# The last item's expert output spread to its tokens on chip, the other items' rows added beside it

## What is computed

```python
logits = (xf @ w_router + b_router).astype(jnp.float32)
top_val, top_idx = lax.top_k(logits, TOP_K)
top_w = jax.nn.softmax(top_val, axis=-1)
comb = jnp.sum(jax.nn.one_hot(top_idx, N_EXPERTS) * top_w[..., None], axis=1)
for e in range(N_EXPERTS):
    hh = xf @ w_expert_in[e] + b_expert_in[e]
    gate = jnp.minimum(hh[:, :D_EXPERT], SWIGLU_LIMIT)
    lin = jnp.clip(hh[:, D_EXPERT:], -SWIGLU_LIMIT, SWIGLU_LIMIT)
    act = (lin + 1.0) * gate * jax.nn.sigmoid(SWIGLU_ALPHA * gate)
    y = y + comb[:, e:e + 1] * (act @ w_expert_out[e] + b_expert_out[e])
...
x = x + gate2(c) * y        # c: one row for the prompt, one for each sample
y_out = rmsnorm(x, final_norm_g)
```

## Time and profile before

| | |
|---|---|
| median of 3 runs | 1531.92 us (1530.77 to 1532.19) |
| the profiled execution, its own time | 1529.73 us |
| its span, first to last instruction | 1528.0 us |
| granted TensorE clock over the span, mean | 0.915 |
| TensorE busy | 1259.7 us, 82% |
| VectorE, ScalarE, POOL busy | 356.3, 307.9, 183.5 us |
| moved by DMA | 534.38 MB, 350 GB/s over the span |
| expert phase, slices of 38.2 us | DMA busy 9 tenths or more in each, 411 to 429 GB/s |

### The profile page before, as it was taken

How to read it: one execution, slowest core, us unless ns; L and a number is a source line. 1 busy time by engine, 2 the same in 40 slices (tenths; PEclk the granted TensorE clock), 3 DMA queues, 4 the chain that set the end, 5 groups by cost and what they waited for, 6 DMA issues and landing times.

```text
span 1528.0 us, 27699 instructions
## 1 busy us (share of the span) xinstructions
PE 1259.7 (82%) x10935; PEld 692.7 (45%) x10936; DVE 356.3 (23%) x756; ACT 307.9 (20%) x638; POOL 183.5 (12%) x300
## 2 busy tenths in 40 slices
PE   6999999999999789999954698496969666954694
PEld 3777887767887434444421243132423222421241
DVE  1023113333631322222211122121222112211123
ACT  3100122442100222222211122121212111211123
POOL 0240100100180001111000011000100000100010
PEclk9999999999999899999987699797989888987697
DMA  9876734999555388799999999999999999999994
GB/s 367 303 286 227 267 111 149 386 371 402 184 179 226 139 342 338 285 419 421 415 427 427 425 412 423 425 419 426 415 418 411 429 423 416 417 429 426 422 411 170
DMA packets 76681, 534.38 MB, mean 350 GB/s; under 512 B 6428, under 2 KB 7540, under 8 KB 49793
## 3 DMA queue, kind: packets, MB, share of 16 engines
q1 hardware_dynamic: 67330, 503.47, 80.5%
q0 software_dynamic: 8928, 29.54, 6.0%
q10 hardware_dynamic: 391, 0.93, 0.2%
HBM read 508.38 MB, written 28.09 MB: 351 GB/s over the span
## 4 chain that ended last, share of the span: by engine, by line
PE 56%; DMA 40%; DVE 2%; SPq 1%; issue 1%; ACT 0%; DVEq 0%; ACTq 0%; POOL 0%; POOLq 0%
DMA ring<-in_w_expert_in_dram 21%; PE ps L754 16%; PE ps L922 12%; DMA moe_ring<-in_w_expert_out_dram 11%; PE ps L946 9%; DMA moe_ring<-in_w_expert_in_dram 5%; PE ps L511 2%; PE ps L891 2%; PE ps L796 2%; PE ps L837 2%; PE ps L803 2%; PE ps L783 2%; DMA ring<-in_w_in_dram 1%; DMA ring<-in_w_ada_dram 1%; PE ps L558 1%; PE ps L637 1%
## 5 line engine op out<-in xcount | busy, mean ns | idle before, releaser
L922 PE MATMUL ps<-ring,xgT 128*32 128x512 f32 x2352 | 318.7, 664 | 179.0 <-DMA ring<-in_w_expert_in_dram 178.5
L754 PE MATMUL ps<-hT,ring 128*128 128x264 f32 x1152 | 268.8, 391 | 6.1 <-DMA ring<-in_w_in_dram 4.7
L754 PEld LDWEIGHTS ps<-hT,ring 128*128 128x128 f32 x1152 | 218.5, 192 | 59.4 <-issue 14.6
L922 PEld LDWEIGHTS ps<-ring,xgT 128*32 128x32 f32 x2352 | 66.2, 116 | 318.3 <-DMA ring<-in_w_expert_in_dram 185.5
L946 PE MATMUL ps<-moe_ring,actT 128*32 128x256 f32 x3136 | 181.7, 380 | 4.7 <-DMA moe_ring<-in_w_expert_out_dram 4.2
L1526 DVE TENSOR_TENSOR xg<-ps,sh_q 128x256 f32<-128x256 f32 x49 | 20.8, 425 | 554.9 <-PE ps L891 554.9
L1164 ACT ACTIVATE ostage<-ps,slots_w 32x256 f32<-32x256 f32 x196 | 91.6, 467 | 285.9 <-PE ps L946 284.1
L946 PEld LDWEIGHTS ps<-moe_ring,actT 128*32 128x32 f32 x3136 | 99.3, 110 | 86.1 <-issue 18.0
L922 PE MATMUL ps<-moe_ring,xgT 128*32 128x512 f32 x784 | 93.7, 595 | 21.3 <-DMA moe_ring<-in_w_expert_in_dram 21.3
L891 PE MATMUL ps<-rows,picked 128*32 128x256 f32 (+1 forms) x1200 | 81.8, 386 | 1.3 <-DVE picked L1481 1.3
L1156 ACT COPY actT<-ps 128x256 f32<-128x256 f32 x49 | 18.3, 373 | 306.7 <-PE ps L511 306.7
(11 more groups left out here) (285 smaller groups left out, 1135.3 us busy)
## 6 DMA issues: line engine op xcount, KB each, us to landing
ring<-in_w_expert_in_dram SPq DMA_DIRECT2D x96, 2048.0 KB, 12.3
moe_ring<-in_w_expert_out_dram SPq DMA_DIRECT2D x64, 2048.0 KB, 12.0
moe_ring<-in_w_expert_in_dram SPq DMA_DIRECT2D x32, 2048.0 KB
ring<-in_w_in_dram SPq DMA_DIRECT2D x18, 2048.0 KB, 12.1
ring<-in_w_ada_dram SPq DMA_DIRECT2D x12, 2048.0 KB, 8.7
ring<-in_state_ret_dram SPq DMA_DIRECT2D x8, 1024.0 KB, 10.8
vslot<-in_state_ret_dram SPq DMA_DIRECT2D x8, 1024.0 KB, 10.8
out_dram<-ring POOLq DMA_DIRECT2D x8, 1024.0 KB, 9.1
```

The costliest lines, as they stand in the source:

```text
L754: mm = nc.tensor.matmul(ps[:, j, 0:T], ring[s][:, k, j * P:(j + 1) * P], hT[:, k, :], start=(k == 0), stop=(k == KC - 1))
L922: mm = nc.tensor.matmul(side(0, g), xgT[:, a, j * SLOTS:(j + 1) * SLOTS], w[:, a, g * COL:(g + 1) * COL], start=False, stop=(j == 3 and a ...
```

## The change

The last item's output is no longer scattered to DRAM and read back. VectorE multiplies its four quarters in PSUM by the slots' weights and by the prompt's gates at once, into `gated` (32 slots by 1024), and TensorE spreads it to the tokens with one-hot matrices `slot_rows` (32 slots by token), which VectorE makes from the item's slot numbers. The sum of the 48 items before is loaded by POOL, not by SP, once their last scatter is in; VectorE multiplies it by the gates and adds it to x1 (`earlier_items`). For the sample tokens, whose gates differ from token to token, ScalarE's `ostage` of the last item is spread ungated, and VectorE multiplies the spread rows by `gate_sample`, which POOL loads early.

The gate matmul for the prompt moves ahead of `outward`, the one for the samples goes. The turned rows of x1 use PSUM bank 5 in place of 1; bank 5 holds the slot numbers of `pick`, so TensorE first waits for `slots_taken`. VectorE's order of the tail becomes add 0, add 1, variance 0, finish 0, variance 1, add 2, finish 1, variance 2, finish 2; ScalarE's stays, with a wait for `out_gated` ahead of `take_outward`.

```diff
@@ SP
-            items = sp.value_load(cum_i[0:1, E - 1:E], min_val=E, max_val=ITEMS)
-            for j in range(2):
-                sp.wait_ge(chunk_used[j], items)
-                sp.sem_inc(paced, 1)
-            sp.wait_ge(rows_free, items + 1)
-            sp.sem_inc(paced, 1)
-            for t, (t0, n) in enumerate(TILES):
-                sp.dma_start(y_in[t][0:n], moe_rows[t0:t0 + n]).then_inc(rows_in[t], 16)
@@ TensorE
-                        mm = turn(ps[0:n, (1, 6, 7)[g % 3], k * P:(k + 1) * P], xT[:, 4 * half + k, t0:t0 + n])
+                        mm = turn(ps[0:n, (5, 6, 7)[g % 3], k * P:(k + 1) * P], xT[:, 4 * half + k, t0:t0 + n])
...
+            pe.wait_ge(slots_taken, SLOT_STEPS * items + SLOT_STEPS)
             rows_turned_back(0, 3)
             turn_hidden(items - 1)
+            pe.wait_ge(hidden_taken, 2 * items + 2)
+            for h in range(2):
+                mm = nc.tensor.matmul(ps[:, h, :], const("selc", NB)[:, 0:P], gate_rows[:, h * COL:(h + 1) * COL], start=True, stop=True)
+            mm.then_inc(rows_spread, 1)
             outward(items - 1, last, True)
 
             pe.wait_ge(x1_copied, 6)
+            pe.wait_ge(out_gated, SIDES)
+            for t in range(2):
+                for h in range(2):
+                    mm = nc.tensor.matmul(ps[:, 3 + 2 * t + h, :], slot_rows[:, t * P:(t + 1) * P], gated[:, h * COL:(h + 1) * COL], start=True, stop=True)
+                mm.then_inc(rows_spread, 1)
+            pe.wait_ge(eo_taken, items + 1)
+            pe.sem_inc(paced, 1)
             for h in range(2):
-                nc.tensor.matmul(ps[:, h, :], const("selc", NB)[:, 0:P], gate_rows[:, h * COL:(h + 1) * COL], start=True, stop=True)
-            for h in range(2):
-                mm = nc.tensor.matmul(ps[0:TS, 6 + h, :], const("selc", NB)[:, TP:T], gate_rows[:, h * COL:(h + 1) * COL], start=True, stop=True)
-            mm.then_inc(gates_spread, 1)
+                mm = nc.tensor.matmul(ps[0:TS, (7, 2)[h], :], slot_rows[:, TP:T], ostage[:, h * COL:(h + 1) * COL], start=True, stop=True)
+            mm.then_inc(rows_spread, 1)
@@ ScalarE
             take_rows(3, 6)
+            act_e.wait_ge(out_gated, SIDES)
             take_outward(items - 1)
@@ VectorE
-            for j in range(2, CHUNKS):
+            for j in range(2):
                 dve.wait_ge(chunk_used[j], items)
             step(nc.vector.memset(small[:, 2:5], 0.0))
-            dve.wait_ge(gates_spread, 1)
+            step(cp(slot_f[:], slots_u[:, bass.ds(items - 1, 1)]))
+            for t, (t0, n) in enumerate(TILES):
+                step(ts(slot_rows[:, t0:t0 + n], const("iota", SLOTS)[:, 0:n], float(t0), slot_f[0:SLOTS, 0:1], ALU.add, ALU.is_equal))
+            gates = ps[:, 0:2, :].rearrange("p b n -> p (b n)")
+
+            def earlier_items(t):
+                n = TILES[t][1]
+                dve.wait_ge(rows_in, 48)
+                step(tt(y_in[t][0:n], y_in[t][0:n], gates if t < 2 else gate_sample[:], ALU.mult))
+                dve.wait_ge(x1_copied, 2 * t + 2)
+                step(tt(x1_rows[0:n, t, :], x1_rows[0:n, t, :], y_in[t][0:n], ALU.add))
+
+            dve.wait_ge(late_in, 32)
+            dve.wait_ge(rows_spread, 1)
+            for g in range(SIDES):
+                side = slice(SLOTS * g, SLOTS * (g + 1))
+                step(cp(gate_side[side], gates[side, g * QUARTER:(g + 1) * QUARTER]))
+            for t in range(3):
+                earlier_items(t)
+            dve.wait_ge(chunk_used[5], items)
+            for g in range(SIDES):
+                side = slice(SLOTS * g, SLOTS * (g + 1))
+                stt(gated[:, g * QUARTER:(g + 1) * QUARTER], ps[side, 2, 0:QUARTER], slots_w[side, bass.ds(items - 1, 1)],
+                    gate_side[side], ALU.mult, ALU.mult).then_inc(out_gated, 1)
+
             def add_rows(t):
-                n = TILES[t][1]
-                bank = 0 if t < 2 else 6
-                gates = ps[0:n, bank:bank + 2, :].rearrange("p b n -> p (b n)")
-                dve.wait_ge(rows_in[t], 16)
-                step(tt(y_out[t][0:n], y_in[t][0:n], gates, ALU.mult))
-                tt(y_out[t][0:n], y_out[t][0:n], x1_rows[0:n, t, :], ALU.add).then_inc(y_added, 1)
+                dve.wait_ge(rows_spread, t + 2)
+                if t < 2:
+                    tt(y_out[t][:], ps[:, 3 + 2 * t:5 + 2 * t, :].rearrange("p b n -> p (b n)"), x1_rows[:, t, :], ALU.add).then_inc(y_added, 1)
+                else:
+                    for h in range(2):
+                        cols = slice(h * COL, (h + 1) * COL)
+                        step(tt(y_out[2][0:TS, cols], ps[0:TS, (7, 2)[h], :], gate_sample[:, cols], ALU.mult))
+                    tt(y_out[2][0:TS], y_out[2][0:TS], x1_rows[0:TS, 2, :], ALU.add).then_inc(y_added, 1)
@@ POOL
             pool.dma_start(g_final[:], final_norm_g.unsqueeze(0).broadcast_to([P, D])).then_inc(late_in, 16)
+            pool.wait_ge(last_rows_ready, 2)
+            pool.dma_start(gate_sample[:], kept_rows[1, 1:NB]).then_inc(late_in, 16)
...
-            scatter(items - 1, None)
+            for j in range(2):
+                pool.wait_ge(chunk_used[j], items)
+                pool.sem_inc(paced, 1)
+            for t, (t0, n) in enumerate(TILES):
+                pool.dma_start(y_in[t][0:n], moe_rows[t0:t0 + n]).then_inc(rows_in, 16)
```

More of the change, by code:

```diff
@@ L277, in trunk_kernel @@
         y_in = [at(f"y_in{t}", [P, D], ring_at + 4096 * t) for t in range(3)]
+        gated = at("gated", [SLOTS, D], ring_at + 28672)
+        slot_rows = at("slot_rows", [SLOTS, T], ring_at + 24576)
+        slot_f = at("slot_f", [P, 1], ring_at + 24576 + size([SLOTS, T]))
+        gate_side = at("gate_side", [P, QUARTER], ring_at + 24576 + size([SLOTS, T]) + size([P, 1]))
+        gate_sample = at("gate_sample", [TS, D], h_at + size([P, D]))
         y_sq = [at(f"y_sq{t}", [P, D], ring_at + 12288 + 4096 * t) for t in range(3)]
@@ L356, in trunk_kernel @@
         last_rows_ready = sem("last_rows_ready")
-        rows_in, gates_spread = [sem(f"rows_in{t}") for t in range(3)], sem("gates_spread")
+        rows_in, rows_spread = sem("rows_in"), sem("rows_spread")
+        out_gated = sem("out_gated")
         y_added, y_squared, y_ready, y_stored = sem("y_added"), sem("y_squared"), sem("y_ready"), sem("y_stored")
@@ L1173, in take_rows @@
                     act_e.wait_ge(x1_turned, g + 1)
-                    nc.scalar.copy(x1_rows[0:n, t, half * COL:(half + 1) * COL], ps[0:n, (1, 6, 7)[g % 3], :]).then_inc(x1_copied, 1)
+                    nc.scalar.copy(x1_rows[0:n, t, half * COL:(half + 1) * COL], ps[0:n, (5, 6, 7)[g % 3], :]).then_inc(x1_copied, 1)
             act_e.wait_ge(moe_cleared, 32)
@@ L1568, in finish_rows @@
                 stt(y_out[t][0:n], y_out[t][0:n], small[0:n, 5 + t:6 + t], g_final[0:n], ALU.mult, ALU.mult).then_inc(y_ready, 1)
-            dve.wait_ge(late_in, 16)
             add_rows(0)
@@ L1573, in _ @@
             variance(0)
+            finish_rows(0)
+            variance(1)
             add_rows(2)
-            variance(1)
-            finish_rows(0)
+            finish_rows(1)
             variance(2)
-            finish_rows(1)
             finish_rows(2)
```

## The result

The changed kernel took 1540.92 us (median of 6, 1536.87 to 1543.34) against 1532.05 for the kernel before (6 runs, 1530.65 to 1533.03): ratio 1.0058, 95% interval 1.0044 to 1.0072. It is slower, as forecast, but by 8.9 us where 5.8 were forecast, and 0.3 us over the upper end of the range. The profiled execution took 1541.72, with a span of 1539.8 (before 1528.0).

The account below looks back on a forecast made before the run. The weight stream was taken to bound the kernel until 1501.4; behind it, loads, VectorE's order and half-clock one-hot pairs, then sums, roots and store, ended at 1533.8 against 1528.0: 5.8 us more, so 1537.7, range 1533.5 to 1540.6.

Parts of the forecast that it names:

- tail: Stretch from VectorE's copy of the last slot weights to the span's end; forecast at 38.1 us.
- first operation on the loaded rows: VectorE's start on the earlier items' rows, once all POOL loads land, at 1503.9.
- gated rows: VectorE's products of the last item, behind all operations on earlier rows; ready at 1513.0.
- The four products: VectorE's gated products of the last item's four quarters, 4 x 0.4 = 1.6 us.
- The pair with its hand-over: TensorE's first pair of one-hot matmuls at half clock, 3.4 us, with 0.1 for handing over.
- The six operations with their hand-over: VectorE's work on three tiles of earlier rows ahead of the gated products, 7.5 us.
- what shifts in 950 us of weight stream: Remaining case: changes ahead of the loop's end that can go either way; 7 in 100.
- the clearing's 4.7 us: POOL's loads timed like the clearing of the same tensor: 4.7 us from issue, bounds 3.8 to 5.6.
- The contention: Loads beside the last weights on the DMAs: would delay the weights little, costed at nothing.
- B: Rival: TensorE's clock returns, one-hot pairs take 1.98 us each; +3.0 us, 1534.9; 15 in 100.
- C: Rival: loads land by 1501.8 and the clock holds, so not slower; +0.9 us, 1532.8; 6 in 100.
- D: Rival: POOL's loads and all behind them come 2.0 us later; +7.8 us, 1539.7; 10 in 100.

Follow-up runs that it names:

- again: The changed kernel once more, unaltered; ratio 1.0043 to the kernel before.
- gates_first: Changed kernel with the prompt's gate matmuls moved ahead of TensorE's wait for the slot numbers and the first turns; ratio 1.0039 to the kernel before.
- sp_loads: Changed kernel with the three loads of earlier rows issued by SP instead of POOL, behind the same scatter; ratio 1.0047 to the kernel before.
- warm: Changed kernel with five unread 128-row matmuls on TensorE between the last output block and the one-hot matmuls; ratio 1.0044 to the kernel before.
- loads_free: gates_first with the rows loaded from input x on ScalarE's queue right behind the loop, without the earlier items' sum; ratio 1.0038 to the kernel before.
- order_only: Changed kernel with only VectorE's order altered: gated products ahead of the operations on loaded rows; ratio 1.0036 to the kernel before.
- warm9: As warm, with nine unread matmuls instead of five; ratio 1.0035 to the kernel before.
- gated_first: order_only and gates_first together, each root right behind its square on ScalarE, variance 0 ahead of sum 1 on VectorE; ratio 0.9987 to the kernel before.

## Why the prediction missed

**The mechanism was right.** Forecast were 5.8 us more, behind the loop only. Term by term, from the slot weights' copy, forecast against the change's profile (and again): first operation on the loaded rows 8.2, measured 8.6 (8.6); gated rows 17.3, measured 18.2 (18.2); first sum 20.8, measured 22.2 (22.1); second sum 24.2, measured 25.6; samples' sum 28.5, measured 29.6; last product done 35.8, measured 36.8; tail 38.1, measured 39.1 (39.0). VectorE's order did hold the gated rows far behind the block, TensorE's spread did begin at half clock, and the samples' square did hold tile 1's root. Against the kernel before, the first operation on rows came 9.8 us earlier, and from there to the end it took 30.5 us instead of 13.9.

**The terms that were too small.** The tail lost 6.8 us, not 5.8. The four products: taken as 4 x 0.4, measured 2.01. The pair with its hand-over: 3.4 + 0.1 between the gated rows and the first sum, measured 3.93. The six operations with their hand-over, 7.5, measured 7.6, and the loads 0.4 later. Together they made the first sum 1.4 late, of which 0.4 came back: from the second sum to the samples' sum the forecast had 4.3 us, and 4.0 were measured.

**The step that failed is the range.** Its top was "the forecast, the loads 2.0 late, and 0.9 for hand-overs that I have left out", 2.9 us over the forecast. It had nothing for the stretch ahead of the loop's end, although the chances named "what shifts in 950 us of weight stream" with 7 in 100. The sum was made against one execution whose copy of the slot weights came at 1495.7, the earliest of all that were profiled; the change's first profile had that copy 5.0 later, and its six runs reach from 1536.87 to 1543.34. The measured median was 3.2 over the forecast: 1.0 by the terms above, 2.1 by what the tail does not explain, and 0.1 by the second median of the kernel before.

Are the 2.1 the change's own? The same kernel, timed again, was 6.6 us slower than before (1.0043), with a tail difference of 6.7. The other kernels with the change's tail (gates_first, sp_loads, warm, loads_free: ratios 1.0039, 1.0047, 1.0044, 1.0038) give 5.8 to 7.2 us, and their tails differ from before by 6.9 to 7.4. Over all twelve timed kernels but order_only, the time by the ratio less the difference of the tails runs from -2.1 (warm9) to +2.1 (the change's first six runs), with a mean of 0.1. So no loss ahead of the loop's end shows; one of under about 1 us is not excluded. The 0.3 us over the range's top were in part chance: with the tail's loss put at 6.8 the same range would have reached 1541.6.

**Wrong reasons that cost nothing here.** The loads were timed from the scatter's landing plus the clearing's 4.7 us, which gave 8.2 and met 8.6 by luck: the first issue came 2.4 us behind the slot weights' copy, not 3.5, and from there the loads took 6.1 us, not 4.7. And loads_free shows that they land there without any scatter. The contention was looked for in the weights only, and costed at nothing; it shows in the loads. And the clock was expected to hold until the block's end. It fell before it in several profiles, so that the block, forecast done at 10.1, was done at 14.2 (again 11.2), and the gate quarters, forecast at 6.1, at 8.5, just when the loads were in; VectorE's order hid both.

**The rivals.** B's mechanism did not occur in the change (7.16 us for the spread at a clock of 0.50), though its price was right. C did not occur, and its premise fell. D did not occur: the loads came 0.4 late, not 2.0. That the change does what it says was so: the 10.6 us are bypassed. They were given back to VectorE's 7.6 us of operations on the loaded rows, which now precede the products, and to the 2.01 us of products and 7.2 us of one-hot matmuls, which are new.

## What to carry to other kernels

Taking a transfer off the path gains nothing if the engine that receives the new data has other work queued ahead of it: put the operation for which another engine waits first, and the work on early data under that engine's time. A sum made from one profile gives a difference; the range for a median must also hold what the unchanged stretch does from run to run, read from more than one execution. An edit that is worth nothing alone (the gates' place) can be part of what makes another pay: VectorE's order alone took the timed ratio from 1.0043 to 1.0036, which the intervals do not tell apart, with the gates' and the roots' place beside it to 0.9987.

## What the runs showed of the hardware that was not expected

- Issued 4.5 us earlier and on another queue, 1.08 MB of loads were in at nearly the same point (8.7 us behind the slot weights' copy in loads_free, 8.8 in gates_first, 9.1 in sp_loads), behind the end of the weight stream.
- TensorE's clock fell while the engine was busy: in gated_first it was 1.00 from 1508 to 1509 and 0.57 in the next microsecond, in the middle of one-hot matmuls of 32 rows that had begun at 1507.44, behind 2.40 us of idle time. In warm9, straight behind 8 us of matmuls of 128 rows, the same ones had a clock of 1.00 for over 2 us before it fell, and took 4.28 us instead of 5.50. What makes it fall was not isolated. Stretches of gated_first:

```profile
1508.00:1509.00 1.00, 1.00 (x4) 0.50 (x3) 0.96 (x2) 0.97 (x3) 0.00 (x0) 1.00 0.03 8
1509.00:1510.00 1.00, 1.00 (x2) 0.33 (x1) 0.97 (x2) 0.97 (x3) 0.00 (x0) 0.57 0.00 0
```

- The same program with the same data had its clock fall at three different places in three runs (order_only), worth 4.6 us.
